# Two stacked transformer blocks on one core: the order of the opening, and four gated tiles that advance together

## What is computed

```python
# first block
mod = silu(c) @ w_ada + b_ada                       # six vectors of 1024, by a 1024 x 6144 matrix
sh_m, sc_m, gt_m, sh_f, sc_f, gt_f = split(mod, 6)
h = rms_norm(x, g_pre_mix) * (1.0 + sc_m) + sh_m
z = h @ w_in + b_in
q, k, v, glu_a, glu_b, gate_a, gate_b = split(z)    # 512, 512, 512, 512, 512, 1024, 1024 columns
u = glu_a * sigmoid(glu_b)                          # the gated tiles: 8 tiles of 128 columns, in 4 pairs
u = causal_dwconv(u, w_dw, b_dw)                    # 31 taps for each channel
...
# second block, for each of its two layers i
h = h + (p_2[i] @ ple_w_2[i]) * gate                # p is 512 x 256, ple_w is 256 x 1024
```

## Time and profile before

| what | value |
| --- | --- |
| median of 3 runs | 1528.09 us (1527.96 to 1529.27) |
| profiled execution | 1527.43 us |
| its span | 1525.6 us |
| TensorE busy | 1433.8 us, 94% |
| VectorE busy | 979.1 us, 64% |
| ScalarE busy | 737.8 us, 48% |
| GpSimd busy | 259.4 us, 17% |
| granted TensorE clock, mean | 0.976 |

### The profile page before, as it was taken

The page is one execution under the profiler, slowest core; times in us unless marked ns, Lnnn a source line. Parts: engine busy times, 40 slices in busy tenths (PEclk is TensorE's granted clock), DMA queues, the critical chain, the costliest instruction groups (busy, mean ns, idle before and its releaser), DMA issues. The chain is left out here.

```text
span 1525.6 us, 19751 instructions
## 1 busy us (share of the span) xinstructions
PE 1433.8 (94%) x6818; PEld 1139.6 (75%) x6818; DVE 979.1 (64%) x1523; ACT 737.8 (48%) x1265; POOL 259.4 (17%) x237
## 2 busy tenths in 40 slices
PE   5899899979989999999999999998999999999996
PEld 3688777768767888887887687776787778888775
DVE  5668877566688656555223757986464568888444
ACT  4425554563454545453113436775444446666432
POOL 3104633231270000000002000111120012232211
PEclk9999999989999999999999999999999999999998
DMA  9533233335522323232222332122222310000321
GB/s 386 222 94 104 83 124 124 107 114 180 208 68 69 110 87 106 82 96 83 96 96 69 99 116 63 49 63 84 82 93 86 97 56 28 29 29 29 124 69 69
DMA packets 39882, 151.67 MB, mean 99 GB/s; under 512 B 4784, under 2 KB 4928, under 8 KB 39040
## 3 DMA queue, kind: packets, MB, share of 16 engines
q1 hardware_dynamic: 29664, 105.92, 21.5%
q0 software_dynamic: 10144, 44.76, 8.2%
HBM read 144.37 MB, written 6.29 MB: 99 GB/s over the span
## 5 line engine op out<-in xcount | busy, mean ns | idle before, releaser
L664 PE MATMUL ps<-a_hi,w_hi 128*128 128x512 f32 x880 | 362.8, 412 | 16.6 <-DVE a_lo L2085 4.7
L665 PE MATMUL ps<-a_lo,w_hi 128*128 128x512 f32 x880 | 350.9, 399 | 0.0
L666 PE MATMUL ps<-a_hi,w_lo 128*128 128x512 f32 x880 | 350.5, 398 | 0.0
L1627 DVE TENSOR_TENSOR w_lo<-w_raw,w_hi 128x1024 fp32r<-128x1024 f32 x126 | 165.8, 1316 | 115.8 <-ACT w_hi L1146 115.3
L664 PEld LDWEIGHTS ps<-a_hi,w_hi 128*128 128x128 f32 x880 | 167.4, 190 | 61.9 <-issue 14.6
L666 PEld LDWEIGHTS ps<-a_hi,w_lo 128*128 128x128 f32 x880 | 167.4, 190 | 40.8
L665 PEld LDWEIGHTS ps<-a_lo,w_hi 128*128 128x128 f32 x880 | 167.8, 191 | 35.5 <-issue 0.5
L1146 ACT ACTIVATE w_hi<-w_raw 128x1024 fp32r<-128x1024 f32 x138 | 144.7, 1049 | 74.4 <-PE ps L666 57.4
L569 POOL TENSOR_TENSOR sq<-sq 128x512 f32<-128x512 f32 x36 | 49.6, 1379 | 531.9 <-ACT sq L1161 531.9
L664 PE MATMUL ps<-b_hi,w_hi 128*128 128x512 f32 x240 | 97.7, 407 | 0.4 <-DVE b_lo L2085 0.4
L666 PE MATMUL ps<-b_hi,w_lo 128*128 128x512 f32 x240 | 94.7, 395 | 0.0
(11 more groups left out here) (340 smaller groups left out, 2997.4 us busy)
## 6 DMA issues: line engine op xcount, KB each, us to landing
w_raw<-in_w SPq DMA_DIRECT2D x198, 512.0 KB, 3.5
ada_a<-in_ada POOLq DMA_DIRECT2D x16, 512.0 KB, 8.0
ada_g<-in_ada POOLq DMA_DIRECT2D x16, 512.0 KB, 3.8
ada_b<-in_ada POOLq DMA_DIRECT2D x16, 512.0 KB, 4.3
x_resid<-in_x POOLq DMA_DIRECT2D x2, 2048.0 KB, 11.9
pl_store<-pl_out POOLq DMA_DIRECT2D x2, 2048.0 KB, 8.7
pl<-pl_store POOLq DMA_DIRECT2D x2, 2048.0 KB, 9.1
alibi<-in_alibi POOLq DMA_DIRECT2D x16, 192.0 KB, 2.7
```

Of the source, the lines that this page charges most:

```text
L664: pe.matmul(o, w[0], r[0], start=start, stop=False, skip_group_check=skip)
L665: pe.matmul(o, w[0], r[1], start=False, stop=False, skip_group_check=skip)
L666: return pe.matmul(o, w[1], r[0], start=False, stop=stop, skip_group_check=skip)
L1627: dve.tensor_tensor(w_lo[:, n % SLOTS, :], raw, hi, ALU.subtract).then_inc(w_lo_done, 1)
```

## The change

Six things are done. (1) GpSimd loads the second p later: behind six `ada_a` loads, with a semaphore of its own; x is loaded behind three `ada_a`, not four. (2) The two stores of `pl_out` leave their place ahead of `u_pad`'s margin and stand behind the `ada_g` loads, where they wait for the first gate product (`R["glu"]` at 1). (3) ScalarE's splits of the weights, of the second p and the squares of x change places. (4) On VectorE the low halves of chunks 0 to 5 and of p stand at other places between the modulation products, one product is ahead of chunk 0, and the first modulation group is finished behind product 13. (5) TensorE sums the first modulation group between the two halves of the second `ple` tiles. (6) `together` is moved up, takes lags, and runs the first four gated tiles abreast (tile 2 one step and tile 3 three steps behind); the halves of chunks 6 and 7 are made between the `a_hi` and `a_lo`, and later gated chunks one chunk further ahead.

```diff
 @block.gpsimd
-            for l in range(2):
-                pool.dma_start(p_raw[:, PT_K * l:PT_K * l + PT_K, :], t_p[l]).then_inc(p_in, 16)
+            def load_p(l):
+                pool.dma_start(p_raw[:, PT_K * l:PT_K * l + PT_K, :], t_p[l]).then_inc(p_in[l], 16)
+
+            load_p(0)
             for u in range(16):
-                if u == 4:
+                if u == 3:
                     pool.dma_start(x[:, :, :], t_x).then_inc(x_in, 16)
...
+                if u == 6:
+                    load_p(1)
...
-            for l in range(2):
-                pool.wait_ge(R["pl"], KT * (l + 1))
-                pool.dma_start(pl_store[l], pl_out[:, KT * l:KT * l + KT, :]).then_inc(pl_saved, 16)
-
             pool.wait_ge(mod_ready, 2)
...
+            pool.wait_ge(R["glu"], 1)
+            for l in range(2):
+                pool.wait_ge(R["pl"], KT * (l + 1))
+                pool.dma_start(pl_store[l], pl_out[:, KT * l:KT * l + KT, :]).then_inc(pl_saved, 16)
 @block.tensor
+            def together(name, src, ready, between=None, lags=(0, 0, 0, 0)):
+
+                def block(j, k):
+                    if k == 0:
+                        free_bank(LT[name] + j)
+                    pe.wait_ge(ready, k + 1)
+                    w = weights(CH[name] + j)
+                    return mm3(ps[:, (LT[name] + j) % LIN, :], cols(w, P * k), (src[0][:, k, :], src[1][:, k, :]), k == 0, k == KT - 1, skip=True)
+
+                for s in range(KT - 2 + max(lags)):
+                    for j in range(LIN):
+                        if 0 <= s - lags[j] < KT - 2:
+                            block(j, s - lags[j])
+                for j in range(LIN):
+                    block(j, KT - 2)
+                    block(j, KT - 1).then_inc(lin_done, 1)
...
-            tiles("ple", KT, (p_hi[:, PT_K:2 * PT_K, :], p_lo[:, PT_K:2 * PT_K, :]), R["p"], PT_K, kt=PT_K, per=4, first=KT)
+            p_last = p_hi[:, PT_K:2 * PT_K, :], p_lo[:, PT_K:2 * PT_K, :]
+            tiles("ple", KT // 2, p_last, R["p"], PT_K, kt=PT_K, per=4, first=KT)
             mod_group(0, acc_a[:, 0, :])
+            tiles("ple", KT // 2, p_last, R["p"], PT_K, kt=PT_K, per=4, first=KT + KT // 2)
             mod_group(1, acc_a[:, 1, :])
-            tiles("glu", 8, A, R["h1"])
+            together("glu", A, R["h1"], lags=(0, 0, 1, 3))
+            tiles("glu", 8 - LIN, A, first=LIN)
 @block.scalar
...
                 act.activation(a_hi[:, k, :], tmp[:, tmps[0] % 2, :], ACT.Identity, bias=mod[:, k:k + 1]).then_inc(hi_done, 1)
                 tmps[0] += 1
+                if k in (0, 2):
+                    split(CH["glu"] + 2 + k // 2)
             for f in range(CT):
                 for j in range(2):
-                    split(CH["glu"] + 2 * f + j + WEIGHT_LEAD)
+                    split(CH["glu"] + 2 * f + j + LIN)
 @block.vector
...
             for u in range(16):
                 mod_unit()
-                if u in (0, 2, 4, 6, 10, 15):
-                    split(1 + (0, 2, 4, 6, 10, 15).index(u))
-                if u == 3:
-                    for k in range(PT_K, 2 * PT_K):
-                        lo(p_lo[:, k, :], p_raw[:, k, :], p_hi[:, k, :], R["p"])
-            mod_group(0)
-            dve.wait_ge(mod_ready, 1)
-            gain(0, "g_pre_mix", 1, 1.0)
+                if u == 0:
+                    split(0)
+                    p_lows(0)
+                if u == 10:
+                    p_lows(1)
+                if u in (1, 8, 11, 13, 15):
+                    split(1 + (1, 8, 11, 13, 15).index(u))
+                if u == 13:
+                    mod_group(0)
+                    dve.wait_ge(mod_ready, 1)
+                    gain(0, "g_pre_mix", 1, 1.0)
             mod_group(1)
...
+                    if k in (1, 3):
+                        split(CH["glu"] + 2 + k // 2)
```

More of the change, by code:

```diff
@@ L693, in tiles @@
                         between(f)
+            def together(name, src, ready, between=None, lags=(0, 0, 0, 0)):
[12 more added lines that the diff above has]
+                    block(j, KT - 1).then_inc(lin_done, 1)
+                    if between is not None:
+                        between(j)
             def token_tiles(tile, chunk, n_chunks, src, width, kt):
@@ L1299, in _ @@
                 ple_out(j)
-                if j == 0:
+                if j == 3:
+                    for k in range(2):
+                        square(x[:, k, :], x_in, 16)
+            for k in range(2, KT):
+                square(x[:, k, :], x_in, 16)
+                if k == 3:
                     split(2)
+                if k == 5:
                     p_part(1)
-                if j == 1:
-                    split(3)
-                if j == 4:
-                    split(4)
-            for k in range(KT):
-                square(x[:, k, :], x_in, 16)
             rsqrt(D)
-            split(5)
+            split(3)
             for j in range(KT, 2 * KT):
                 ple_out(j)
+                if j == KT + 1:
+                    split(4)
                 if j == KT + 4:
-                    split(6)
+                    split(5)
             for k in range(KT):
@@ L1340, in _ @@
             for f in range(8):
-                split(CH["qk"] + f + WEIGHT_LEAD)
+                if f:
+                    split(CH["qk"] + f + WEIGHT_LEAD)
                 if f == 0:
```

25 lines of the change are left out of this document (5 added, 20 removed).

## The result

The changed kernel takes 1517.88 us (median of 4 runs, 1517.24 to 1518.71); the kernel before took 1528.68 in the same session. The ratio is 0.993, with a 95% interval of 0.9918 to 0.9941. The profiled execution took 1517.88 us against 1527.43: 9.55 less, where 9.5 had been worked out. By the medians of the session the gain is 10.80 us.

A forecast was written before the change was run, and what follows sets the result against it. TensorE sets the end of the opening, held up by chains of queues, not bandwidth alone. Gated tiles 8.45 us earlier plus 1.05 shorter make 9.5 us: 1517.9 profiled, 1518.6 as median, range 1515.6 to 1523.4.

The forecast's parts named there:

- First matmul: TensorE's start: one modulation product goes first on VectorE, so 11.9 instead of 10.99 us, a loss of 0.9.
- First eight tiles and squares: Opening on TensorE: projection tiles to 25.4 us without the 2.89 hole, then eight sums of squares in 8.2, to 33.6.
- Second tiles: Second eight projection tiles wait 0.5 us for product 10 and p_lo, start at 34.1, take 11.3.
- rival that the loads pace it: Opening: waits only move; product 10 comes 3 us later and everything behind it too, total 1521.6; chance 0.12.
- 4 MB of other traffic left: Opening: an argument against loads setting the pace, that the pl_out stores no longer share the DMA engines there.
- Modulation: Modulation matmuls, 1.84 and 2.07 us, done at 49.3; VectorE's last split at 45.1, cover 2.2.
- First gated matmul: Start of the gated tiles: 52.1 instead of 60.55 us, earlier by 8.45.
- Four tiles: First four gated tiles abreast: 25.0 us, then TensorE waits 1.2 for bank 0; 2.6 by the skill page's drain.
- Gated tiles as a whole: All eight gated tiles on TensorE: 48.6 us instead of 49.7, shorter by 1.05.
- Last sigmoid of the gated tiles: Sign at the end of the gated tiles on ScalarE: near 100.8 us instead of 110.24.
- Stores: pl_out stores start near 77.5 us beside weight loads and cost nothing, the first needed chunk being some 10 us ahead.
- Given back before attention: Rival at attention 1: VectorE's taps nearly 5 us later in phase; if 3 us remain, 1521.6; chance 0.14.

The follow-up runs named there:

- e6: Changed kernel with the loads of x and of the second p back in the order of before; 1519.65 us.
- e2: Changed kernel with the two stores of pl_out back at their old, earlier place; 1517.49 us.
- e1: Changed kernel with TensorE's eight gated tiles one after the other again instead of four abreast; 1521.12 us.
- e8: Changed kernel with both pl_out stores made twice, the second pair behind the landing of the first; 1519.71 us.
- e11: e10 with ScalarE's first sigmoid and VectorE's first gate product ahead of the split of chunk 9; 1521.48 us.
- e12: e11 with the two stores of pl_out back at their old, earlier place; 1516.28 us.
- e10: e9 with convolution taps on VectorE moved from beside the v tiles to beside the gated tiles; 1515.80 us.
- e4: Changed kernel with both modulation groups summed behind the last ple tile, VectorE using the first behind product 15; 1520.20 us.
- e3: Kernel before with only the four gated tiles abreast and the splits that needs; 1527.76 us.
- e5: Changed kernel with ScalarE's sigmoid table loaded right behind the last a_hi; 1517.64 us.
- e9: e5 with chunk 0's split and first p_lo ahead of the first modulation product, second p_lo behind the tenth; 1517.31 us.

## Why the prediction was right, point by point

- **First matmul.** 11.9 forecast, 11.57 measured. e6 prices the moved p load at 0.9 to 1.4 us (1.4 in the working).
- **First eight tiles and squares.** The sums were to start at 25.4 and do at 24.76. No wait for x: the squares run at 19.85, right behind the fourth copy. The eight sums take 8.4 us (8.2).
- **Second tiles.** Forecast at 34.1 behind the tenth product with a wait of 0.5; they start at 33.16 with 0.21. The rival that the loads pace it did not come about. One reason given against it was misread: "4 MB of other traffic left" does not bear on it, for the first store was issued at 37.47, behind all loads that product 10 needs.
- **Modulation.** Done at 48.06, not 49.3. Apart from the 0.9 us inherited, the second group took 1.84 us at a clock of 1.00, not the 2.07 of the trace before, at 0.89. VectorE's last split ends at 45.0 (45.1).
- **First gated matmul.** 50.79, not 52.1: 9.76 us earlier, not 8.45. This term was 1.3 us too small, from small errors that all had one sign. Part of it is the execution: this one is the earliest of five with the same opening (50.79 to 51.67).
- **Four tiles.** 25.42 us and a wait of 1.26, where 25.0 and 1.2 stood. The wait is what was worked out step by step. Between the load of the table and the sigmoid lie 1.30 us (74.58 to 75.88), as in the earlier trace rows; the drain that the Trainium skill (ScalarE: Activation LUTs, "What ACT_TABLE_LOAD costs") adds is not there, so the row decided rightly. The 2.6 us that followed from the page did not come.
- **Gated tiles as a whole.** Here a term was mis-sized: "shorter by 1.05". From first gated matmul to q copy it is 55.35 us before and 55.05 after: 0.30 us. TensorE alone says the same: from the first gated matmul to the first of the q tiles it is 49.49 us before (60.55 to 110.04) and 49.19 after (50.79 to 99.98), where 49.7 and 48.6 stood. The old figure was 0.2 too long, since it ran to the sigmoid at 110.24. The new one was 0.6 too short, and 0.5 of that lies ahead of tile 4: 26.68 us, not 26.2. The forecast had "some 10 of them slow" and 0.7 us of waits. There was no wait, but in the changed kernel the first 13 intervals between matmuls are 0.42 us or more, in e2 only the first 7, each some 0.2 us or more above the 0.233 of the higher clock. So with the same instructions e2 needs 53.69 us to the q copy, 1.66 less than before: the size of this term is no better known than about 1.4 us. And the working compared the new tiles with the old ones; it did not ask what the new splits would cost the old way of running them. That is e1's answer: 3 us.
- **Last sigmoid of the gated tiles.** This sign was missed: 102.09, not near 100.8, and 2.1 us behind TensorE, which had left the gated tiles by 99.98. ScalarE was held by the weights (9.52 us before 92.34), and the sigmoids stand behind the splits.
- **Stores.** Issued at 77.71 (77.5 forecast). Priced at nothing, and nothing they cost, though weight loads beside them took 11.5 us. But the reason given, some 10 us of lead, was too comfortable. Chunk 12's high half is made at 92.34 to 93.4 and its low half by 94.7, and it is used at 99.98, so 5 us are left. The bank has less: tile 8, the first q tile, needs bank 0, which tile 4 holds until the third gate product is made (97.51 to 98.25, behind the split of chunk 13), and so 1.7 us are left. The working had followed the weights and not the bank behind them; e8 and e11 show that it is the bank where TensorE then waits (1.46 and 3.74 us). Whether their move was needed depends on the rest: not in e2, by 0.25 us, and for 0.7 us in e12.
- **Given back before attention.** Not at all: 3.88 us. VectorE caught up behind the gated tiles (63.41 of 67.80 us busy, not the 57.98 of 67.20 in the earlier trace rows). e10 says that its taps do count at this place.
- **What the hit owes to luck.** The opening gave 10.06, 0.56 more than the 9.5 forecast: 1.31 too little was forecast up to the first gated matmul and 0.75 too much behind it. Behind attention's start the clock gave 1.11 and took 1.35 us, and 0.3 us more are lost in the last 11 us of the span, a stretch that takes 10.4 to 11.5 us in the 14 profiled executions. None of these four was forecast, and they cancel to 0.05 us.

## What to carry to other kernels

In an opening, price the order of each in-order queue first: one engine stood 6 to 8 us for one operand with ready work behind it, and moving that work was worth 8 of 10 us, while reordering transfers was worth 1 to 2 and holding stores back 0 to 0.7. A change that frees a bank earlier can release a large transfer earlier too; if that transfer is tied to an event instead of a place among the loads, each later tuning moves it over them. When a weight load comes late, look for the bank that waits behind it in the same queue: it can run out before the weights do. And judge edits of a microsecond by marks in the trace right behind the edit, since the same gap further down may cost 1.35 us more or less from one execution to the next.

## What the runs showed of the hardware

**The granted clock behind one and the same gap.** Near the end TensorE stands for 2.51 us in every kernel. Before, then changed:

```profile
1423.40 0.50 PE L664 MATMUL ps<-a_hi,w_hi 128*128 128x512 f32 x1 [2.51 <-POOL a_lo L612]
1423.74 0.39 PE L665 MATMUL ps<-a_lo,w_hi 128*128 128x512 f32 x1
```

```profile
1412.23 0.79 PE L668 MATMUL ps<-a_hi,w_hi 128*128 128x512 f32 x1 [2.51 <-POOL a_lo L616]
1412.82 0.63 PE L669 MATMUL ps<-a_lo,w_hi 128*128 128x512 f32 x1
```

The same matmul on the other side of the gap takes 0.39 us in one (clock 1.00) and 0.63 in the other (1.2 of 2.4 GHz). From this gap to the last idle time it is 91.09 us before and 92.44 after. In the 14 profiled executions it was 91.1 in four (before, e4, e6, e11) and 92.4 to 92.7 in ten. None of the edits touches that place. What decides it was not found.

**Matmuls of one column.** A group of 16 sums of one column took 1.84 us at a granted clock of 1.00 (38.83, 46.22), 2.07 at 0.89 (before, 55.70) and 3.02 at 0.59 (e4, 47.15). So the clock shows in them too. All three of the second groups that followed another within 0.35 us (before, e3, e4) were slower than 1.84, by 0.08 to 1.18 us.

**Weight loads beside a 2 MB transfer.** 512 KB issued next behind the two stores took 11.0 to 11.5 us (changed kernel, e1, e5, e8 to e11), and 12.8 and 13.5 beside e8's second pair. Issued ahead of the stores they took 4.7 to 5.7 us in the changed kernel, e5 and e8, but 9.2 and 9.5 in e9 and e10, with a lead of only 0.8 us. With no store beside them it was 3.4 to 4.6 (e2, e12).
